# A transformer layer on one Trainium2 core: GpSimd's down operations in parts, ScalarE's first chunk in another order, and a new order of the last thirteen products and of the outputs

## The reference, cut to what matters

```python
hf = rms_norm(x, g_ffn)
x = x + (jax.nn.silu(hf @ w_gate) * (hf @ w_up)) @ w_down   # 1024 -> 2816 -> 1024
...
y = rms_norm(x, g_final)        # y * rsqrt(mean(y * y) + eps) * g, all in float32
```

## Time and profile before

| | before |
|---|---|
| median of 3 runs | 806.49 us (806.28 to 807.29) |
| the profiled execution, its own time | 806.45 us |
| its span, first to last instruction | 804.7 us |
| mean granted TensorE clock | 0.995 of full speed |
| busy: TensorE, VectorE, ScalarE, GpSimd | 97%, 69%, 56%, 56% of the span |

### The profile page before, as it was taken

How to read it: one execution, slowest core, us unless ns; L and a number is a source line. 1 busy time by engine, 2 the same in 40 slices (tenths; PEclk the granted TensorE clock), 3 DMA queues, 4 the chain that set the end, 5 groups by cost and what they waited for, 6 DMA issues and landing times.

```text
span 804.7 us, 16014 instructions
## 1 busy us (share of the span) xinstructions
PE 783.2 (97%) x5739; PEld 744.6 (93%) x5739; DVE 559.2 (69%) x1050; ACT 454.5 (56%) x865; POOL 450.4 (56%) x327
## 2 busy tenths in 40 slices
PE   7999999999999999999999999999999998999995
PEld 6987998888888999998999999999999998999995
DVE  6354367887779736457589776766767688888784
ACT  7462565666677334554466555555555665556464
POOL 3665963383214555740465545445764488999945
PEclk9999999999999999999999999999999999999998
DMA  8342432111025333330123233322333122132213
GB/s 265 106 137 95 156 99 69 35 37 37 28 80 185 118 105 106 109 126 28 40 96 108 74 105 104 102 62 96 104 104 103 58 100 98 61 105 92 79 41 118
DMA packets 26506, 75.93 MB, mean 94 GB/s; under 512 B 2880, under 2 KB 7432, under 8 KB 26312
## 3 DMA queue, kind: packets, MB, share of 16 engines
q1 hardware_dynamic: 25888, 74.28, 28.6%
q10 hardware_dynamic: 560, 0.88, 0.3%
HBM read 68.62 MB, written 6.53 MB: 93 GB/s over the span
## 4 chain that ended last, share of the span: by engine, by line
PE 87%; DVE 4%; issue 3%; ACT 3%; POOL 2%; DMA 1%; SPq 0%; POOLq 0%; DVEq 0%; ACTq 0%
PE ps L1173 14%; PE ps L1174 13%; PE ps L1175 13%; PE ps L649 13%; PE ps L651 12%; PE ps L650 12%; PE ps L808 2%; PE ps L826 2%; PE ps L667 1%; PE ps L1078 1%; ACT whi L1311 1%; POOL wlo L2580 1%; DMA wraw<-w_front 1%; PE ps L675 1%; PE ps L791 1%
## 5 line engine op out<-in xcount | busy, mean ns | idle before, releaser
L1311 ACT ACTIVATE whi<-wraw 128x512 fp32r<-128x512 f32 (+3 forms) x150 | 112.8, 755 | 92.7 <-PE ps L1175 46.4
L649 PE MATMUL ps<-hhi,whi 128*128 128x288 f32 x480 | 144.3, 301 | 5.8 <-DVE hlo L1866 5.7
L2731 POOL TENSOR_TENSOR wlo<-wraw,whi 128x512 fp32r<-128x512 f32 x63 | 86.9, 1394 | 106.5 <-ACT whi L1311 106.5
L650 PE MATMUL ps<-hhi,wlo 128*128 128x288 f32 x480 | 142.7, 297 | 0.0
L651 PE MATMUL ps<-hlo,whi 128*128 128x288 f32 x480 | 142.6, 297 | 0.0
L2580 POOL TENSOR_TENSOR wlo<-wraw,whi 128x256 fp32r<-128x256 f32 (+2 forms) x83 | 89.7, 1108 | 83.9 <-ACT whi L1311 83.7
L1173 PE MATMUL ps<-hhi,whi 128*128 128x288 f32 x380 | 112.2, 295 | 2.1 <-ACT sqacc L1311 1.5
L1174 PE MATMUL ps<-hhi,wlo 128*128 128x288 f32 x380 | 111.9, 295 | 0.0
L649 PEld LDWEIGHTS ps<-hhi,whi 128*128 128x128 f32 x480 | 91.1, 190 | 7.5 <-DVE hlo L1866 5.6
L1175 PE MATMUL ps<-hlo,whi 128*128 128x288 f32 x320 | 94.4, 295 | 0.0
L650 PEld LDWEIGHTS ps<-hhi,wlo 128*128 128x128 f32 x480 | 90.9, 189 | 0.2
(11 more groups left out here) (372 smaller groups left out, 2253.9 us busy)
## 6 DMA issues: line engine op xcount, KB each, us to landing
wraw<-w_ff SPq DMA_DIRECT2D x44, 512.0 KB, 4.1
wraw<-w_front SPq DMA_DIRECT2D x41, 512.0 KB, 3.7
wraw<-w_down SPq DMA_DIRECT2D x16, 512.0 KB, 4.1
wraw<-w_down SPq DMA_DIRECT2D x8, 384.0 KB, 3.6
wraw<-w_front SPq DMA_DIRECT2D x7, 384.0 KB, 3.5
xa<-x_t SPq DMA_DIRECT2D x8, 288.0 KB, 5.1
xs<-x_t SPq DMA_DIRECT2D x7, 288.0 KB, 5.2
out_y<-xb SPq DMA_DIRECT2D x3, 576.0 KB, 3.1
```

Of the source, the lines that this page charges most:

```text
L649: nc.tensor.matmul(out, lh, rh, start=start, stop=False)
L650: nc.tensor.matmul(out, ll, rh, start=False, stop=False)
L1311: return nc.scalar.activation(out, src, func, **kw)
L2731: g.tensor_tensor(w_operand(1, j), src, f(w_operand(0, j)), ALU.subtract).then_inc(g_lo, 1)
```

## The change

GpSimd's turns are made in two instructions instead of one, its low parts in four (first chunk) or two. ScalarE makes the high part of (0, 3) ahead of that of (0, 4), and that of (0, 5) at the end of window G; GpSimd makes the low part of (0, 5) ahead of the remainder of (1, 0). In the last steps the products (11, 1) and (11, 3), and (10, 4) and (11, 5), change places; VectorE's and ScalarE's orders follow; squares of the first tile pair and the root's first use (which loads its table) move up; the low half's sums go in front of (11, 4) and its broadcast in front of (11, 6). The outputs are made and stored in seven pieces instead of five, and GpSimd makes two tiles of each half instead of four and two.

```diff
-        ENDING = [(LA, 2), (LA, 1), (LB, 0), (LA, 3), (LB, 2), (LA, 5), (LB, 1), (LB, 3), (LA, 4), (LB, 5), (LA, 6), (LB, 4),
+        ENDING = [(LA, 2), (LA, 1), (LB, 0), (LA, 3), (LB, 2), (LA, 5), (LB, 3), (LB, 1), (LB, 5), (LA, 4), (LA, 6), (LB, 4),
                   (LB, 6)]
...
-        HIGH = [(0, 0), (0, 2), (0, 1), (0, 4), (0, 3), (0, 5), (0, 6), (1, 0), (1, 4), (1, 2), (1, 1), (1, 6), (1, 3), (1, 5),
+        HIGH = [(0, 0), (0, 2), (0, 1), (0, 3), (0, 4), (0, 5), (0, 6), (1, 0), (1, 4), (1, 2), (1, 1), (1, 6), (1, 3), (1, 5),
...
             def last_columns(half):
-                after(pe, e_acc, 5 + 2 * half)
-                for n0, source in enumerate((sqacc[:, 0:T], hidf[:, 15, :], hidf[:, 14, :])):
-                    if n0:
-                        after(pe, e_sq, 4 if half == 0 else 5 + n0)
+                sources = ((hidf[:, 15, :], e_sq, 4), (hidf[:, 14, :], e_sq, 4), (sqacc[:, 0:T], e_acc, 5)) if half == 0 else \
+                    ((sqacc[:, 0:T], e_acc, 7), (hidf[:, 15, :], e_sq, 6), (hidf[:, 14, :], e_sq, 7))
+                for n0, (source, signal, count) in enumerate(sources):
+                    after(pe, signal, count)
...
             for s, j in ENDING:
-                if (s, j) == (LB, 6):
+                if (s, j) == (LB, 4):
                     last_columns(0)
+                elif (s, j) == (LB, 6):
+                    last_rows(0)
                 down(s, j, LAST_BANK.get((s, j)))
-            last_rows(0)
             last_columns(1)
             last_rows(1)
...
                 op_high(3, p)
                 if last:
+                    hidden_high(0, 3)
                     hidden_high(0, 4)
-                    hidden_high(0, 3)
                     down_a21(1)
...
                 op_high(5, p)
+                if last:
+                    hidden_high(0, 5)
...
                         down_a21(s + 2)
                         if s == LA - 1:
+                            pair_squares(0)
+                        elif s == LA - 2:
                             activation(small[0:96, S_LSD:S_LSD + 1], small[0:96, S_EPS:S_EPS + 1], ACT.Sqrt)
...
             for j in (1, 2, 4, 6):
                 down_high(LB, j)
-            pair_squares(0)
             down_high(LB, 3)
             pair_squares(1)
             down_high(LB, 5)
+            half_squares(4, 6, x_low, ((LA, "x2"), (LA, "x6")))
             after(act, e_sq, 2)
-            for m in range(4):
+            for m in range(3):
                 gains_on(m, slice(0, T))
-            half_squares(4, 6, x_low, ((LA, "x2"), (LA, "x6")))
-            half_squares(6, 8, x_low, ((LB, "x6"),))
+            half_squares(6, 8, x_low, ((LB, "x2"), (LB, "x6")))
+            gains_on(3, slice(0, T))
...
             half_squares(4, 6, x_high, ((LA, "x7"),))
+            last_root(0)
             half_squares(7, 8, x_high, ((LB, "x5"),))
-            last_root(0)
+            last_row(0)
             half_squares(6, 7, x_high, ((LB, "x7"),))
-            last_row(0)
...
             x3(LA)
-            down_sums(LB)
+            down_sums_2_6(LB)
+            x1(LB)
             down_low(LB, 2)
-            x1(LB)
+            down_sum_3(LB)
+            x4(LA)
             x2(LA)
-            x4(LA)
+            down_low(LB, 3)
+            x3(LB)
             down_low(LB, 4)
-            x3(LB)
-            down_low(LB, 3)
             x6(LA)
             down_low(LB, 6)
+            x4(LB)
             x2(LB)
-            x4(LB)
+            x6(LB)
             x5(LA)
             x8(LA)
-            x6(LB)
             x7(LA)
-            x5(LB)
-            x8(LB)
...
             reciprocals(0)
+            x5(LB)
+            x8(LB)
+            outputs(0, 0, 2)
             x7(LB)
-            outputs(0)
+            outputs(0, 2, 6)
             reciprocals(1)
-            outputs(1)
+            outputs(1, 0, 2)
+            outputs(1, 2, 4)
...
-                g.tensor_tensor(src[j], a, b, ALU.subtract).then_inc(h_turn[0], 1)
+                for k in (slice(0, 2), slice(2, D_KN[c])):
+                    mm = g.tensor_tensor(src[j][:, k, :], a[:, k, :], b[:, k, :], ALU.subtract)
+                mm.then_inc(h_turn[0], 1)
...
-                g.tensor_tensor(D_LO[c][j], D_SRC[c][j], f(D_HI[c][j]), ALU.subtract).then_inc(h_lopool[0], 1)
+                parts = 4 if c == 0 else 2
+                for n in range(parts):
+                    k = slice(n * D_KN[c] // parts, (n + 1) * D_KN[c] // parts)
+                    mm = g.tensor_tensor(D_LO[c][j][:, k, :], D_SRC[c][j][:, k, :], f(D_HI[c][j])[:, k, :], ALU.subtract)
+                mm.then_inc(h_lopool[0], 1)
...
-            MADE_AT = {(0, 0): ((hidden_low, 0, 5), (hidden_low, 0, 6)), (1, 1): ((hidden_turn, 1, 4), (hidden_turn, 1, 3)),
+            MADE_AT = {(0, 0): ((hidden_low, 0, 6),), (1, 1): ((hidden_turn, 1, 4), (hidden_turn, 1, 3)),
...
             for s in range(LA):
-                if s == 4:
+                if s == 0:
+                    hidden_low(0, 5)
+                elif s == 4:
                     hidden_low(1, 3)
...
             down_rest(LB, 0)
+            squares_added(0, whole, 1, 1)
             down_rest(LB, 1)
-            whole = slice(0, T)
-            squares_added(0, whole, 1, 1)
...
-            outputs(0, 4)
+            outputs(0, 6)
             outputs(1, 6)
...
-            for signal, count, j0, j1, cc in ((s_y, 1, 0, 4, x_low), (s_yp, 1, 4, 8, x_low), (s_y, 2, 0, 4, x_high),
-                                              (s_y, 4, 4, 6, x_high), (s_yp, 2, 6, 8, x_high)):
+            for signal, count, j0, j1, cc in ((s_y, 1, 0, 2, x_low), (s_yp, 1, 6, 8, x_low), (s_y, 2, 2, 6, x_low),
+                                              (s_y, 3, 0, 2, x_high), (s_y, 4, 2, 4, x_high), (s_yp, 2, 6, 8, x_high),
+                                              (s_y, 6, 4, 6, x_high)):
```

More of the change, by code:

```diff
@@ L414, in build @@
                       (s, "x4"), (s + 1, "low2"), (s + 1, "x1"), (s + 1, "low4"), (s + 1, "low3"), (s, "x6")]
-        D_VEC += [(LA - 1, "x7"), (LA, "low6"), (LB, "s4"), (LA, "x3"), (LB, "s2"), (LB, "s6"), (LB, "s3"), (LB, "low2"), (LB, "x1"),
-                  (LA, "x2"), (LA, "x4"), (LB, "low4"), (LB, "x3"), (LB, "low3"), (LA, "x6"), (LB, "low6"), (LB, "x2"), (LB, "x4"),
-                  (LA, "x5"), (LA, "x8"), (LB, "x6"), (LA, "x7"), (LB, "x5"), (LB, "x8"), (LB, "x7")]
+        D_VEC += [(LA - 1, "x7"), (LA, "low6"), (LB, "s4"), (LA, "x3"), (LB, "s2"), (LB, "s6"), (LB, "x1"), (LB, "low2"), (LB, "s3"),
+                  (LA, "x4"), (LA, "x2"), (LB, "low3"), (LB, "x3"), (LB, "low4"), (LA, "x6"), (LB, "low6"), (LB, "x4"), (LB, "x2"),
+                  (LB, "x6"), (LA, "x5"), (LA, "x8"), (LA, "x7"), (LB, "x5"), (LB, "x8"), (LB, "x7")]
         T_NEEDS = {0: 1, 1: 4, 2: 4, 3: 2, 4: 3, 5: 4, 6: 3}
@@ L1781, in _ @@
             window((G, None))
-            HIGH_AT = {(0, 6): ((0, 5),), (0, 0): ((0, 6),), (1, 0): ((1, 0),), (2, 0): ((1, 4),), (2, 1): ((1, 2),), (2, 3): ((1, 1),),
+            HIGH_AT = {(0, 0): ((0, 6),), (1, 0): ((1, 0),), (2, 0): ((1, 4),), (2, 1): ((1, 2),), (2, 3): ((1, 1),),
                        (3, 0): ((1, 6),), (3, 1): ((1, 3),), (3, 3): ((1, 5),), (5, 0): ((2, 0),), (5, 1): ((2, 1),),
@@ L1791, in _ @@
                     down_high(s, 6)
-                for made in HIGH_AT.get((s, 6), ()):
-                    hidden_high(*made)
                 for j in (0, 1, 2, 4, 3, 5):
@@ L2440, in down_sum_4, with down_sums_2_6 @@
                 v.tensor_tensor(down_sum(s, 4), ps[:, 7, 0:down_w(s)], down_raw(s, 1, 1), ALU.add).then_inc(d_vec[0], 1)
-            def down_sums(s):
-                a11, a12, a21 = down_raw(s, 0, 0), down_raw(s, 0, 1), ps[:, 7, 0:down_w(s)]
+            def down_sums_2_6(s):
+                a11, a12 = down_raw(s, 0, 0), down_raw(s, 0, 1)
                 after(dve, d_vec, vec_at(s, "s4"))
@@ L2448, in down_sums, with down_sum_3 @@
                 v.tensor_tensor(down_sum(s, 6), a12, down_sum(s, 2), ALU.subtract).then_inc(d_vec[0], 1)
-                v.tensor_tensor(down_sum(s, 3), a11, a21, ALU.subtract).then_inc(d_vec[0], 1)
+            def down_sum_3(s):
+                v.tensor_tensor(down_sum(s, 3), down_raw(s, 0, 0), ps[:, 7, 0:down_w(s)], ALU.subtract).then_inc(d_vec[0], 1)
             def down_low(s, j):
@@ L2502, in _ @@
                     x3(s)
-                down_sums(s + 1)
+                down_sums_2_6(s + 1)
+                down_sum_3(s + 1)
                 x2(s)
@@ L2548, in reciprocals, with outputs @@
                     .then_inc(n_rc, 1)
-            def outputs(half):
+            def outputs(half, m0, m1):
                 cc = (x_low, x_high)[half]
@@ L2553, in outputs @@
                 dve.wait_ge(n_row, 6 + 2 * half)
-                dve.wait_ge(s_xg, 4)
-                v.tensor_tensor(xb[:, 0:4, cc], xb[:, 0:4, cc], row.unsqueeze(1).to_broadcast([128, 4, HT]), ALU.mult)\
+                dve.wait_ge(s_xg, 4 if m1 <= 4 else 8)
```

(15 more changed lines are left out.)

## The result

The changed kernel takes **808.13 us** (median of 22 runs, 806.92 to 813.9) against 807.0 for the kernel before (22 runs): a ratio of 1.0022, 95% interval 1.0014 to 1.003. It is slower by 0.2%, where 0.1% faster was forecast. Its profiled execution took 808.25 us, with a span of 806.4.

The account below looks back on a forecast made before the run. TensorE, busy 783.2 of 804.7 us, was taken as the bound, with time to win only in its waits and the tail. +0.2 + 0.3 + 0.5 - 1.9 = -0.9 from 806.45 gave 805.55, rounded to 805.4 us; range 802.6 to 807.4.

Parts of the forecast that it names:

- ScalarE's first chunk: First chunk of the down product: earlier high parts of (0, 3) and (0, 5) remove GpSimd's two waits for ScalarE, -3.36 us.
- fourth rival: First chunk: the joined wait of 4 us lets TensorE's clock fall, one product at half speed, 807.2 us; chance 0.06.
- A part was to take 0.775: GpSimd's four-part operations: 0.775 us a part, four parts 3.10 where a whole operation takes 2.66.
- second rival: GpSimd's parts are paced like lone operations with a handover at each, 0.91 us a part: +3.8, 810.3 us; chance 0.10.
- The first chunk was to lose 0.2: First chunk of the down product: -3.36 + 2.64 + 0.9 = +0.2 us, bounds -2.5 and +1.3.
- 0.9 for handovers: First chunk: VectorE operations that now run between GpSimd's parts add 0.9 us to GpSimd's chain, bounds 0 and 1.2.
- 0.44 charged for each: First chunk: each GpSimd operation made in four parts costs 0.44 us more than whole; six of them, 2.64 us.
- (2, 3), +0.3: Product (2, 3): the two-part turns of step 1 delay VectorE's turn and the addition it waits for, +0.3 us.
- The second chunk, +0.5: Second chunk: four split operations in GpSimd's gapless work up to 722.04 cost +0.5 us, bounds 0 and 0.8.
- The end, -1.9: Last products and outputs: earlier low-half outputs and last broadcast end the kernel 1.9 us sooner, bounds -0.25 and -2.4.
- third rival: The tail doesn't move, because the outputs are bound by the transfers: +1.0, 807.4 us; chance 0.08.
- first rival: VectorE and ScalarE bound the first chunk and parts are nearly free: -4.4, 802.1 us, halfway 803.5; chance 0.32.

Follow-up runs that it names:

- remainder first: The changed kernel with GpSimd again making the remainder of (1, 0) ahead of the low part of (0, 5), as in the kernel before: 806.48 us.
- filled: The changed kernel, its order kept, with 22 matmuls of overwritten result ahead of product (1, 0), in TensorE's long wait: 806.25 us.
- no parts, remainder first: The changed kernel with GpSimd's turns and low parts whole and the remainder of (1, 0) ahead of the low part of (0, 5): 805.36 us.

## Why the prediction was wrong

The sum was -0.9; the traces of the changed kernel give +0.5 and its median +1.1. The step that failed is in **ScalarE's first chunk**: "TensorE, through (0, 3) by 671, waits there nearly 4 us in one piece, and then runs (1, 0), (0, 5) and (0, 6) without a stop". The wait came as worked out (3.77), but joining waits was priced at nothing ("The small waits join into one"). What follows ran at 1.2 GHz for over 3 us and lost 1.5. With the wait cut (remainder first, -0.77) or filled (-0.96), the traces stand where the forecast put them; the medians (-0.27 and -0.50) lie some 0.5 above, which belongs to the last paragraph of this section.

The cause was my fourth rival, and its chance of 0.06 was the mistake behind the step. I took the clock for safe because it held through idle times up to 1.46 us; but my own sum made a wait more than twice as long, for which no row stood. The rival's own price, one product at half speed, 1.8 us, was near the 1.5 measured. The rule of the Trainium skill, page "TensorE: Matmul & The Clock Gate" (section What's actually happening), that the lower clock is the default and activity lifts it, is borne out by these runs: 22 matmuls without any use kept the clock at 1.00.

The other steps, read from the kernel with the remainder first (0.27 us taken off for its landmark, 159.35 against 159.08), with three more waits of it:

```profile
695.98 0.37 PE L1173 MATMUL ps<-hhi,whi 128*128 128x288 f32 x1 [0.25 <-DVE xb L2467]
...
719.12 0.37 PE L1173 MATMUL ps<-pb,whi 128*128 128x288 f32 x1 [0.52 <-DVE s L2451]
...
723.16 0.37 PE L1173 MATMUL ps<-hlo,whi 128*128 128x288 f32 x1 [0.62 <-issue]
```


- A part was to take 0.775: four take 3.06 to 3.09, 0.77 each; the second rival (0.91 a part) is out. The first chunk was to lose 0.2: (0, 6) starts at 677.96 - 0.27 = 677.69, against 677.78, so it won 0.1. The 0.9 for handovers is right only in sum, and that by luck: the two operations that VectorE came between grew from 3.19 and 3.72 to 4.30 and 4.99, 1.5 more than the 0.44 charged for each, but the two remainders behind the first of them took 0.7 less (2.53 for 3.21).
- (2, 3), +0.3: 695.98 - 0.27 against 695.52 is +0.2, which is +0.3 behind the 0.1 won. Right.
- The second chunk, +0.5: 723.16 - 0.27 against 722.14 is +0.75, 0.55 of it new. The size is right, but the place only in part: the delay stands already at 719.12 in that kernel (721.62 above), where a product waits 0.52 us for VectorE's sum of weights.
- The end, -1.9: measured alone, -1.98. The last broadcast is 0.2 earlier, and from it to the end 1.8 less. The third rival is out.
- The first rival, VectorE as the bound and parts nearly free: half of it is true. Without parts VectorE is the bound; but the parts are not free, so the gain came only where parts were left out.

The page "SBUF — State Buffer" of the Trainium skill (section Who interferes with whom) says that a VectorE instruction with two SBUF inputs contends with a GpSimd instruction that reads SBUF. The rows agree: the same VectorE operation takes 3.17 us beside a whole GpSimd operation and 1.29 beside parts.

The rest of the 1.1 us in the medians is not settled. Both traces of the changed kernel are the latest of all twelve at the landmark (160.31 and 160.10; the others 158.67 to 159.82), in code that is the same; and where all parts stay, 2 of 22, 2 of 12, 1 of 11 and 2 of 12 runs took 4 us or so more than the rest, which widens those intervals; no other kernel's runs did, and no trace here shows one. The granted clocks point to more time at the lower level: of the changed kernel's first 22 executions, the twelve at 0.994 or 0.995 took 806.92 to 808.33 us, eight at 0.991 to 0.993 took 807.9 to 809.34, and the two long ones had 0.989 and 0.991. Where in the kernel that time lies is not shown.

## What to carry to other kernels

A wait has a shape as well as a sum: before an order of work joins short waits of TensorE into one, look whether any row shows a wait that long with the clock at its upper level, and if none does, price the work behind it at the lower level. Such a wait can be cut by making first what TensorE needs first, or filled with matmuls whose result is overwritten. Cut a long GpSimd operation only where VectorE is seen to lie behind it: two of the split operations carried the gain here, the others only paid for it.

## What was not expected of the hardware

A TensorE wait of 2.02 us, with a wait of only 0.30 us ahead of it in that chunk's second half, was followed by matmuls at the lower clock in the traced execution (no parts, remainder first), though probably not in every one; three waits of 0.80, 1.24 and 1.20 us, one product apart, were not (remainder first). And where the slow stretch lies differs between executions of one kernel: from 1.3 us behind the wait in the first trace, at once in the second, for about the same loss.
